# Opening of a two-layer block: modulation rows in pairs with two projection chunks tile by tile, and gate rows two places later

## The reference, cut to what matters

```python
mod = jax.nn.silu(c) @ ada_w[i] + ada_b[i]
sh_a, sc_a, g_a, sh_f, sc_f, g_f = jnp.split(mod[:, None, :], 6, axis=-1)
h = rms_norm(x, attn_norm[i]) * (1.0 + sc_a) + sh_a
...
mq, mk, mv, nq, nkv, ng = jnp.split(h @ w_in, SPARSE_SPLITS, axis=-1)
# per head: rms_norm and partial rotation of queries and keys, then block, compressed,
# selected and window attention, then o @ w_out, x + g_a * y, the gated FFN, and so on
```

## Time and profile before

| | us |
|---|---|
| median of 3 executions | 2203.2 (2202.68 to 2203.76) |
| the profiled execution: its own time | 2204.52 |
| its span on the core | 2202.7 |
| TensorE busy | 2156.7 (98%) |
| weight loads busy | 1899.7 (86%) |
| VectorE busy | 1847.5 (84%) |
| ScalarE busy | 1327.0 (60%) |
| GpSimd busy | 112.2 (5%) |
| chain that ended last, by engine | PE 82%, DVE 12%, DMA 3%, issue 2%, ACT 1% |

### The profile page before, as it was taken

How to read it: one execution, slowest core, us unless ns; L and a number is a source line. 1 busy time by engine, 2 the same in 40 slices (tenths; PEclk the granted TensorE clock), 3 DMA queues, 4 the chain that set the end, 5 groups by cost and what they waited for, 6 DMA issues and landing times.

```text
span 2202.7 us, 31747 instructions
## 1 busy us (share of the span) xinstructions
PE 2156.7 (98%) x12960; PEld 1899.7 (86%) x12960; DVE 1847.5 (84%) x2321; ACT 1327.0 (60%) x1495; POOL 112.2 (5%) x155
## 2 busy tenths in 40 slices
PE   6999999999999999999999999999999999999998
PEld 4888999889999979999888888888888888888886
DVE  7967888876998677888896988989897988989896
ACT  3574433575343776434633777777777777777775
POOL 3000111000010000100000000000000000000021
PEclk9999999999999999999999999999999999999999
DMA  9855988625887616885643899999998999999992
GB/s 370 299 190 201 344 314 316 230 77 211 305 299 276 225 39 239 325 325 179 227 171 136 325 372 370 365 345 363 370 358 343 369 365 371 368 345 357 373 360 85
DMA packets 137360, 633.30 MB, mean 288 GB/s; under 512 B 9304, under 2 KB 21625, under 8 KB 115194
## 3 DMA queue, kind: packets, MB, share of 16 engines
q1 hardware_dynamic: 112698, 536.83, 64.9%
q0 software_dynamic: 24512, 94.38, 11.4%
HBM read 630.13 MB, written 1.05 MB: 287 GB/s over the span
## 4 chain that ended last, share of the span: by engine, by line
PE 82%; DVE 12%; DMA 3%; issue 2%; ACT 1%; SPq 0%; DVEq 0%; ACTq 0%
PE ps L1266 80%; DVE wring_rounded L3211 3%; DMA aring<-in_ada_rows 3%; DVE aring L3238 2%; DVE work L3211 1%; PE ps L2391 1%; DVE OT L3235 1%; PE ps L1469 1%; DVE F L3218 1%; DVE F L3211 0%; PE ps L1444 0%; DVE work L3750 0%; ACT scr_rounded L2472 0%; ACT F_rounded L2472 0%; DVE work_rounded L3211 0%
## 5 line engine op out<-in xcount | busy, mean ns | idle before, releaser
L3211 DVE TENSOR_TENSOR wring_rounded<-wring,scr_rounded 128x2048 fp32r<-128x2048 f32 (+1 forms) x314 | 569.6, 1845 | 58.2 <-ACT scr_rounded L2472 57.8
L2472 ACT ACTIVATE scr_rounded<-wring 128x2048 fp32r<-128x2048 f32 (+1 forms) x314 | 479.7, 1553 | 181.8 <-PE ps L1266 125.3
L1266 PE MATMUL ps<-wring_rounded,OT_rounded 128*128 128x512 f32 (+1 forms) x1184 | 314.8, 390 | 2.6 <-DVE wring_rounded L3211 1.7
L1266 PEld LDWEIGHTS ps<-wring_rounded,OT_rounded 128*128 128x128 f32 x1184 | 220.1, 188 | 47.2 <-DVE wring_rounded L3211 2.3
L3238 DVE CUSTOM_DVE_ANT_0 aring<-aring,F,vec 128x1024 f32<-128x1024 f32 x152 | 187.9, 1283 | 35.6 <-DMA aring<-in_ada_rows 34.8
L3211 DVE TENSOR_TENSOR wring_rounded<-wring,H_rounded 128x2048 fp32r<-128x2048 f32 (+1 forms) x85 | 193.9, 2281 | 24.2 <-ACT H_rounded L2472 24.0
L3211 DVE TENSOR_TENSOR wring_rounded<-wring,aring_rounded 128x2048 fp32r<-128x2048 f32 x84 | 193.4, 2302 | 12.4 <-ACT aring_rounded L2472 12.1
L2472 ACT ACTIVATE H_rounded<-wring 128x2048 fp32r<-128x2048 f32 (+1 forms) x85 | 162.3, 1910 | 54.7 <-issue 38.4
L2472 ACT ACTIVATE aring_rounded<-wring 128x2048 fp32r<-128x2048 f32 x84 | 161.2, 1919 | 54.4 <-PE ps L1266 54.4
L1266 PE MATMUL ps<-V_rounded,wring_rounded 128*128 128x256 f32 x1184 | 177.9, 285 | 4.6 <-DVE wring_rounded L3211 4.6
L1266 PE MATMUL ps<-work_rounded,F_rounded 128*128 128x256 f32 x1056 | 169.8, 283 | 0.0
(11 more groups left out here) (391 smaller groups left out, 3695.8 us busy)
## 6 DMA issues: line engine op xcount, KB each, us to landing
wring<-in_moe_gate SPq DMA_DIRECT2D x56, 2048.0 KB, 8.5
wring<-in_moe_up SPq DMA_DIRECT2D x56, 2048.0 KB, 9.0
wring<-in_moe_down SPq DMA_DIRECT2D x56, 2048.0 KB, 8.6
aring<-in_ada_rows POOLq DMA_DIRECT2D x88, 1024.0 KB, 7.5
wring<-in_ffn_w_gate SPq DMA_DIRECT2D x10, 2048.0 KB, 11.0
wring<-in_ffn_w_up SPq DMA_DIRECT2D x10, 2048.0 KB, 15.3
wring<-in_ffn_w_down SPq DMA_DIRECT2D x10, 2048.0 KB, 10.5
wring<-in_diff_w_in SPq DMA_DIRECT2D x6, 2048.0 KB, 15.3
```

The costliest lines, as they stand in the source:

```text
L1266: return pe.matmul(dst, lhsT, rhs, start=start, stop=stop, **kw)
L2472: return act.activation(dst, src, ACT.Copy, **kw)
L3211: return ve.tensor_tensor(dst, x, y, op)
```

## The change

SP's loads stand in another order: the small ones and X first, then eight times a buffer of modulation rows followed by one tile (128 rows) of two chunks' weights, columns 2048 to 2560 and 1536 to 2048. A buffer now holds the shift rows and the scale rows of one tile. DVE makes the sine tables' arguments first, then for each tile the two sums, the scale, the rest of the tile before, and the rests of two weight slices. POOL multiplies X by the root, ACT scales, shifts and rounds a tile and rounds two slices. TensorE makes 12 products for each tile, with six idle products ahead. The chunk of 280 columns comes third. `row_squares`, `rows` and `turn_rows` follow the new order. `add_more(0)` and `add_more(1)` stand where 2 and 3 stood, and 2 to 5 where 4 and 5 stood.

The diff, cut to what the prediction speaks of:

```diff
+                if n == 6:
+                    sp.wait_ge(ada_used, 1)
+                sp.dma_start(ada0_buffer(n), first_rows[:, n]).then_inc(ada0_loaded[n], 16)
+
+            def load_slices(k, loaded):
+
+                for j, lo in enumerate((2048, 1536)):
+                    sp.dma_start(slice_weights(j, k, False), w[k * P:(k + 1) * P, lo:lo + CH]).then_inc(loaded, 16)
 
...
-            for h, loaded in enumerate((first_half_loaded, sp_w[0].sem)):
-                sp.dma_start(wring[:, sp_w[0].slot, h * 2048:(h + 1) * 2048].rearrange("p (k n) -> p k n", n=CH),
-                             w[h * 512:(h + 1) * 512, 2048:2560].rearrange("(k p) n -> p k n", p=P)).then_inc(loaded, 16)
+            load_first(0)
+            for k in range(1, KT):
...
+            norm_spread[0].emptied(pool)
+            for k in range(KT):
+                pool.tensor_tensor(H[:, k, :], X[:, k, :], rstd[:], ALU.mult).then_inc(by_root, 1)
...
-            pe.wait_ge(ada_used, 7)
-            idle_products(3, 14)
-            by_token_split(sp_w[0], 0, sp_tok[0], CH, OTupper, Hlower, HI_TILES[0])
+            idle_products(3, 12)
+            for job in sp_tok[0] + sp_tok[1]:
+                job.open(pe)
+
+            def slice_products(k):
+
+                def run(x, lower, last):
+
+                    for j in range(2):
+                        wk = slice_weights(j, k) if lower else slice_part(j, k)
+                        for qt, job in enumerate(sp_tok[j]):
+                            ins = mm(PS[job.b][:, :], x[:, k, qt * P:(qt + 1) * P], wk,
+                                     k == 0 and x is OTupper and not lower, last and k == KT - 1)
+                            if last and k == KT - 1:
+                                fill(job, ins)
+                    return ins
+
+                idle_products(3, 6)
+                pe.wait_ge(hi_tile, k + 1)
+                pe.wait_ge(slice_upper, 2 * k + 2)
+                run(OTupper, False, False)
+                pe.wait_ge(slice_lower, 2 * k + 2)
+                run(OTupper, True, False)
+                pe.wait_ge(lo_tile, k + 1)
+                ins = run(Hlower, False, True)
+                if k < KT - 1:
+                    ins.then_inc(slice_used, 1)
+
+            pe.sem_inc(part_used, 3)
+            for k in range(KT):
+                slice_products(k)
+            pe.sem_inc(part_used, 1)
             pe.wait_ge(con_loaded, 16)
-            by_token_split(sp_w[1], 2, sp_tok[1], 280, OTupper, Hlower)
-            by_token_split(sp_w[2], 4, sp_tok[2], CH, OTupper, Hlower, None, lambda: turn_rows(sp_turn[1], 2))
+            by_token_split(sp_w[2], 4, sp_tok[2], 280, OTupper, Hlower)
+            turn_rows(sp_turn[1], 0)
             by_token_split(sp_w[3], 6, sp_tok[3], CH, OTupper, Hlower, None, lambda: turn_rows(sp_turn[2], 4))
...
-            for n in range(1, 3):
-                round_part(sp_w[n // 2], n, 280 if n == 2 else CH)
+            norm_spread[0].filled(act)
+            copy(rstd[:], PS[norm_spread[0].b][:, 0:T]).then_inc(norm_spread[0].bank.free, 1)
+            act.sem_inc(part_upper_made, 4)
+
+            def shifted_tile(k):
+
+                act.wait_ge(scaled, k + 1)
+                act.wait_ge(by_root, k + 1)
+                scale, shift = gsc[:, k:k + 1], mod[:, 0, k:k + 1]
+                affine(OTupper[:, k, :], H[:, k, :], scale, shift).then_inc(hi_tile, 1)
+                affine(H[:, k, :], H[:, k, :], scale, shift).then_inc(x_shifted, 1)
+
+            def round_slices(k):
+
+                slice_loaded(act, k)
+                if k >= 2:
+                    act.wait_ge(slice_used, k - 1)
+                for j in range(2):
+                    copy(slice_part(j, k), slice_weights(j, k, False)).then_inc(slice_upper, 1)
+
+            for k in range(KT):
+                shifted_tile(k)
+                round_slices(k)
+            round_part(sp_w[2], 4, 280)
             act.wait_ge(con_loaded, 16)
+            sp_tok[1][1].filled(act)
+            round_part(sp_w[2], 5, 280)
+            row_squares(sp_tok[1], 8)
+            row_roots(0, 8)
 
             def rounds(j):
                 for n in (2 * j + 3, 2 * j + 4):
...
+            turned_rows(sp_turn[1], (F[:, 8:12, :], vc("nsa_q_rest")), (other_queries[:, 4:8, :], vc("nsa_q_rest", 1)))
+            round_part(sp_w[3], 7)
...
                 last.then_inc(job.bank.free, 1)
-            sp_turn[1][1].emptied(act)
+            sp_turn[2][1].emptied(act)
             for par in range(2):
                 for g in range(2):
                     for half in range(2):
                         last = copy(*window(par, g, half, 1))
             last.then_inc(windows_ready, 1)
             row_squares(sp_tok[3], 8)
+            round_part(sp_w[4], 9)
             row_roots(6, 8)
-            rounds(3)
-            turned_rows(sp_turn[2], (F[:, 8:12, :], vc("nsa_q_rest")), (other_queries[:, 4:8, :], vc("nsa_q_rest", 1)))
+            round_part(sp_w[5], 10)
...
 
-                ve.wait_ge(ada0_loaded[n], 16)
-                add_rows(ada0_buffer(n), 0, 2 * n, crow)
+                ve.wait_ge(ada0_loaded[n], 3 * 16 if n else 16)
+                w, o = ada0_buffer(n), VEC["ada_b"][0] + n
+                for m in range(2):
+                    last = ve.tensor_tensor_reduce(w[:, m, :], w[:, m, :], crow, 1.0, vec[:, o + KT * m:o + KT * m + 1],
+                                                   ALU.mult, ALU.add, mod[:, 0, n + KT * m:n + KT * m + 1])
+                last.then_inc(ada_used, 1)
+
+            def scale_tile(k):
+
+                ve.wait_ge(ada_used, k + 1)
+                o = VEC["attn_norm"][0] + k
+                stt(gsc[:, k:k + 1], mod[:, 0, KT + k:KT + k + 1], 1.0, vec[:, o:o + 1], ALU.add, ALU.mult).then_inc(scaled, 1)
+
+            def slice_rest(j, k):
+
+                ve.wait_ge(slice_upper, 2 * k + j + 1)
+                tt(slice_weights(j, k), slice_weights(j, k, False), slice_part(j, k).bitcast(F32), ALU.subtract).then_inc(
+                    slice_lower, 1)
+
+            def lower_tile(k):
+
+                ve.wait_ge(x_shifted, k + 1)
+                tt(Hlower[:, k, :], H[:, k, :], OTupper[:, k, :].bitcast(F32), ALU.subtract).then_inc(lo_tile, 1)
 
             def add_more(n):
 
...
+            for job in crow_job:
+                job.emptied(ve)
+            add_first(0)
+            scale_tile(0)
+            for k in range(1, KT):
+                add_first(k)
+                if k == 1:
+                    inverse(0)
+                scale_tile(k)
+                lower_tile(k - 1)
+                for j in range(2):
+                    slice_rest(j, k - 1)
+            lower_tile(KT - 1)
+            for j in range(2):
+                slice_rest(j, KT - 1)
+            part_rest(sp_w[2], 4, 280)
+            part_rest(sp_w[2], 5, 280)
             ve.wait_ge(rotary_made, 4)
             ve.wait_ge(con_loaded, 16)
+            row_sums(0, 8)
+            rows(0, sp_tok[1], 8, ((0, 0, 8, 4),), None)
 
             def rests(j):
                 for n in (2 * j + 3, 2 * j + 4):
                     if n < 12:
-                        part_rest(sp_w[n // 2], n, 280 if n // 2 == 1 else CH)
-
-            part_rest(sp_w[1], 2, 280)
-            add_more(0)
-            row_sums(0, 8)
-            rows(0, sp_tok[0], 8, ((0, 0, 2, 5), (4, 4, 2, 6)), None)
-            rests(0)
-            row_sums(2, 2)
-            rows(2, sp_tok[1], 2, ((0, 6, 2, 7),), None)
-            rests(1)
-            add_more(1)
-            row_sums(4, 8)
-            rows(4, sp_tok[2], 8, ((0, 0, 8, 4),), sp_turn[1])
-            rests(2)
-            sp_turn[1][1].emptied(ve)
+                        part_rest(sp_w[n // 2], n)
+
+            row_sums(2, 8)
+            part_rest(sp_w[3], 6)
+            rows(2, sp_tok[0], 8, ((0, 0, 2, 5), (4, 4, 2, 6)), sp_turn[1])
+            part_rest(sp_w[3], 7)
+            row_sums(4, 2)
+            rows(4, sp_tok[2], 2, ((0, 6, 2, 7),), None)
+            part_rest(sp_w[4], 8)
+            sp_turn[2][1].emptied(ve)
             for par in range(2):
                 for g in range(2):
                     for half in range(2):
@@ -3640,16 +3731,16 @@
             row_sums(6, 8)
             rows(6, sp_tok[3], 8, ((0, 0, 8, 2),), sp_turn[2])
             rests(3)
-            add_more(2)
+            add_more(0)
             for b in range(2):
                 ve.tensor_copy(Cl[0:HD, b * T:(b + 1) * T], F[HD:P, 13 + b, :])
                 last = ve.tensor_copy(Cl[HD:P, b * T:(b + 1) * T], F[0:HD, 13 + b, :])
             last.then_inc(ksw_ready, 1)
-            add_more(3)
+            add_more(1)
             row_sums(8, 8)
             rows(8, sp_tok[4], 8, ((0, 0, 8, 3),), sp_turn[3])
             rests(4)
-            for n in range(4, 6):
+            for n in range(2, 6):
                 add_more(n)
```

(34 more changed lines are left out.)

77 lines of the change are left out of this document (32 added, 45 removed).

## The result

The changed kernel took 2220.56 us (median of 4 runs, 2219.20 to 2221.26) against 2203.48 (2202.68 to 2204.01) before: a ratio of 1.0077, 95% interval 1.006 to 1.0095. It is 17 us slower, where +1.2 was forecast. The span grew by 15.5 us in the profiled executions, 2202.7 to 2218.2.

A forecast was written before the change was run, and what follows sets the result against it. TensorE was taken as bound for 82% of the span, after an opening bound by loading modulation rows. 3.2 won and 4.2 lost gave +1.1 to 1.2 us: 2204.4 median, 2205.7 profiled; 8-in-10 range 2199.5 to 2208.5.

The forecast's parts named there:

- To the root: Opening loads and root: second buffer of rows landed at 15.9, root ready at 15.9, TensorE at 19.3.
- the first rival: Opening: TensorE's clock falls in its 2.7 us gap before the spread; 3.2 later, launch 2207.5; chance 0.17.
- The stages: Opening: eight stages, TensorE the narrow bound at 4.0 each against VectorE's 4.22, the last ending at 54.0.
- Covered, unless it exceeds 3: Opening: GpSimd's product of 1252 ns, one tile wanted each 4 us, costs nothing unless it exceeds 3.
- its head start: Opening: VectorE's slower work, first stage waiting until about 22.1, ends at 50; its last rests are wanted at 53.
- 59 us: Opening: end if VectorE lost up to 1.25 a tile beside GpSimd for all eight; launch about 2209.5.
- Second turn, last turn: TensorE after the opening: second turn ends at 73.5, 4.2 won; last turn at 108.7, 3.2 won.
- Gate rows: VectorE ahead of attention: two load waits, first maximum 117.8; TensorE waits 4.2, turning first weights at 121.6; 4.2 lost.
- Behind it only shifts: After the first attention turn: units run at TensorE's pace as before, so nothing is caught up or lost.
- my own signs of being wrong: Included clock 0.50 after 18 us, first attention turn before 119 or after 124, and a difference arising behind 125 us.

The follow-up runs named there:

- the bank experiment: Changed kernel with gate rows spread, window products' result moved from bank 6 to 2 and last chunk's from 2 to 6: 2206.05 us, ratio 1.0011.

## Why the prediction was wrong, step by step

**Bound and method.** That TensorE is the bound from the second turn on, and that the gate rows would eat the gain, held. The size did not.

**To the root.** Second buffer forecast 15.9, came 16.88; TensorE at 19.3, came 19.52. Right within 1 us. The clock did fall there (0.50 from 20 to 22), the first rival, but cost nothing: without a fall, in the run with 17 idle products, the stages took the same (39.40 from a spread at 18.64, against 58.84 - 19.52 = 39.32).

**The stages: failed.** "Covered, unless it exceeds 3" was the failed step for GpSimd's product. All eight stand one behind the other at 1.07, not one each 4 us, and VectorE paid for them in its first two stages. The first product came at 25.44 instead of 23.2 (19.3 + 2.6 + 1.3 for six more idle products), and 58.84 instead of 54.0 was the end; taking GpSimd away gives 2.6 of these 4.8 back in one trace and 1.7 in the mean. The rest is the root's way to the first product (24.61 there, still 1.4 late) and VectorE's pace, 4.15 a stage there and 4.24 in the changed kernel. VectorE's pace itself was forecast right, at 4.22; what failed is that its head start would cover it, so that TensorE with 4.0 would be the bound. The Trainium skill (SBUF — State Buffer, "Who interferes with whom") says that a VectorE instruction with two SBUF inputs contends with a GpSimd one that reads SBUF; the trace agrees in both directions, and not as a whole instruction lost: 1.76 instead of 1.28 for a sum, where a product of GpSimd takes 1.07. I had its rule, put 59 us beside it, and gave it no chance of its own. That 58.84 is close to this 59 is luck: 59 took a loss in all eight stages, and the trace has it in the first two.

**Second turn, last turn.** Forecast 4.2 and 3.2 won; measured 0.7 and 1.8 lost (the second turn ended at 78.42 against 77.68, the last at 112.66 + 1.07 = 113.73 against 111.93). The bank that the window products share with the fourth chunk (0.69, and 2.25 in one experiment) I did not see: the change's (0, 4, 2, 6, 0, 2), the line that the bank experiment takes out, said it.

**Gate rows.** Forecast: two waits of VectorE, first maximum at 117.8. It came at 122.90: 3.6 since VectorE was at buffer 2 at 107.04 instead of 103.4, and 1.5 since a third wait came, for a load that was issued at 100.38, just behind SP's load of `w_out` (100.08), and took 10.45 instead of 5.25. From the maximum to the turn 3.8 were forecast and 3.95 came, and the 4.2 us of TensorE's wait came as 4.14. The mechanism was right, with the opening's error added.

**"Behind it only shifts": failed, and this is the larger half.** I named the clock as a rival for the gap of 2.7 us in the opening and did not ask it of the 4.2 us wait that I forecast myself. Two of my own signs of being wrong came: the first attention turn after 124, and a difference that arises behind 125 us. It costs 4.2 us there and, with the two places behind, about 7; filling the waits brings 9.9 back, which takes in a fall that the kernel before has too. The Trainium skill (TensorE: Matmul & The Clock Gate, "Why this matters for your kernels") warns of idle gaps between bursts; the trace agrees, and for shorter gaps than the page warns of: behind two waits of 2.14 and 2.00 with 2 us of small products between, and behind one of 2.36 in an experiment, the clock fell.

## What to carry to other kernels

A wait that you predict for TensorE has two prices: its length, and the lower clock for work behind it; ask for the second at each wait that you forecast, fill the wait with idle products first, and take these out again once the wait is gone, since 17 of them cost 3.9 us of TensorE's own time. The kernel before still pays 1.5 us for a fall behind its wait of 1.32 near 310; no run here fills that wait. Before work is moved, look at which engine takes the late pieces (here 5 us of sums put ahead of a memset that TensorE waits for) and at which bank each result gets. A helper engine is not free (GpSimd's products made VectorE's sums 1.76 us instead of 1.28 while they overlapped): give it its work while the other is idle.

## What the runs showed of the hardware

In the run with the root on VectorE the clock stayed at 0.50 for 47 us while TensorE was busy in every one of them, nearly all of it in the mix of 30-column and 512-column products (a 30-column group of four took 0.89 instead of 0.52). The same mix, entered without a wait (77.75 to 111 in the run with the banks changed) or behind the same wait of 0.69 in the changed kernel, ran at 1.00 throughout. So such a wait can be followed by a fall and need not be. Runs of one kernel, that with the gate rows spread, differed by it: 2216 and 2231, where the mean granted clock was 0.995 and 0.986. With the root on VectorE, GpSimd's 128x16 products took 0.22 while VectorE was idle, and also while it multiplied X by the root, with one of its two inputs in PSUM; beside a sum, with both inputs in SBUF, they took up to 1.25, the length of a sum.
